# One transformer block with a 128 x 128 expert table: odd weight builds of the second half scaled by VectorE, two heads of u rows beside them, and routing pieces between the last tile's residual sums

## The chip, the cores and the metric

One core of a Trainium2 chip. TensorE (PE) multiplies matrices, VectorE (DVE) and ScalarE (ACT) work on rows of 128 partitions, GpSimd (POOL) issues the indirect gathers, SyncE (SP) issues the plain loads. The metric is device time in microseconds of one launch.

## The reference

Two blocks run on 512 tokens of width 1024. The first is pooling plus forgetting attention. The second is two attentions followed by an expert layer, `peer_ffn`, and the change lies in that layer:

```python
def block(xt):                                   # 128 tokens
    q = (xt @ w_q).reshape(128, 8, 2, 128)
    sc = einsum('thcd,chnd->thcn', q, sub_keys)  # 2 x 128 scores a head
    top_s, top_i = top_k(sc, 16)
    cand_s = top_s[:, :, 0, :, None] + top_s[:, :, 1, None, :]
    cand_i = top_i[:, :, 0, :, None] * 128 + top_i[:, :, 1, None, :]
    best_s, best_pos = top_k(cand_s.reshape(128, 8, 256), 16)
    idx = take_along_axis(cand_i..., best_pos)   # 16 of 16384 experts
    g = softmax(best_s)
    pre = einsum('td,thkd->thk', xt, u[idx])
    coef = g * gelu(pre)
    return einsum('thk,thkd->td', coef, v[idx])
```

Each token and head picks 16 experts, takes the dot product with their u rows, and sums their v rows with the weights `coef`. Everything is float32, so one gather of a row for 128 tokens moves 512 KB.

## The kernel before, in words

There are four tiles of 128 tokens and eight heads, so 32 chunks k = 8*tile + head, with 16 rows each. Two tiles at a time go through the dense layers and the attentions. Then the expert layer has its own stages.

**Routing.** `prep_top(k)` on VectorE finds the 16 experts of a chunk, in seven pieces with a `yield` after each. They are taken from one stream, `experts()`. In the attention code `side(n)` takes the next n pieces of the stream. `combine(i, n)` adds one of four projections to the residual of tile i, `prep_norm` norms it, and TensorE then projects the queries (the `pq` weights).

**Chunks 0 to 15 (tiles 0 and 1).** Their u rows are gathered and dotted (`dots`) during the dense work. Their v part is not gathered: TensorE multiplies the whole v table, 128 tiles of 128 rows, by a dense matrix of weights. The matrix is made in two halves of 64 tiles. For each half there are 32 builds. `picks(b)` on VectorE makes two one-hot operands for 8 tokens, `pick_a` (128 x 512) and `pick_j` (128 x 1024). ScalarE multiplies `pick_a` by the weights (`scaled`, eight instructions of 128 x 64). TensorE multiplies the two (`build`), and ScalarE copies the product out of PSUM (`spread`). Operands and PSUM banks are doubled: `picks(b)` waits for build b-2. After the 32 builds of a half, `dense(i)` runs its 64 tiles.

**Chunks 16 to 31 (tiles 2 and 3).** Their u and v rows are both gathered. GpSimd issues them in the fixed order `SEQ`, one queue, strictly in turn, and `wait_buffer` holds each until its buffer is free. Chunks 16 and later use a ring of 12 row buffers (`row_ring`), until v24. So a gather waits until the row twelve places ahead of it in the order has been used. A u row is freed by VectorE's dot product, a v row of chunks 16 and 17 by TensorE (`weighted`, with a diagonal made by ScalarE), a later v row below 24 by VectorE (`added`). From v24 on more buffers serve.

**Second half of the builds.** TensorE does one build and one v row of chunks 16 and 17 in turn, 32 of each. VectorE does `picks`, and in the first eight builds also two dots of u24. GpSimd's order is u24, v16, v17, u25, v18, u26, v19 and so on.

**After it.** VectorE walks `SEQ`. At each u chunk that is not in `WITH_SECOND` it first routes up to three more heads (`k_top < k + 5`), then does the dots. After every u chunk, also one in `WITH_SECOND`, it calls `weigh` for chunks up to k-2. `weigh(k)` waits for ScalarE's Exp and Gelu of that chunk, and ScalarE does the pair for chunk k at the place of u(k+1) in `SEQ`. So it does the pair of chunk 23 right after its last `spread` of the builds.

In the text below "build 40" means counting both halves, so the second half is builds 32 to 63. "v row 0 to 31" counts the rows of v16 and v17 together, and row n follows build 32+n.

## Time and profile before

| | us |
|---|---|
| median of 3 runs | 2355.33 |
| lowest, highest | 2352.23, 2360.59 |
| profiled execution | 2354.88 |
| its span, first to last instruction | 2353.0 |

So 1.88 us lie around the span. Busy over the span: PE 83%, DVE 63%, POOL 42%, ACT 23%, and the DMA engines move 261 GB/s on average. In 40 slices, each digit a tenth:

```profile
PE   6999999987498998987887799999899999503466
DVE  0111124453888884679974889988366867786644
DMA  5322335065487687797886773899774999999998
```

A slice is 59 us. The builds of the first half run at about 1346 to 1462, the first 64 tiles to 1684, the second builds to 1814, the last 64 tiles to 2031. After that only row gathers are left.

### The profile page before, as it was taken

Reading aid. Unit: us, or ns where it says so; the run is one execution under the profiler, and the core shown is the slowest. Engines: PE = TensorE matmul, PEld = TensorE weight load, DVE = VectorE, ACT = ScalarE, POOL = GpSimd, SP = SyncE. Lnnn points to the kernel's source line nnn. Section 1 sums busy time; section 2 is a strip of 40 time slices with the busy share of each in tenths; the row PEclk is TensorE's granted clock in tenths of the full one; section 3 lists DMA queues with packets and bytes.
Section 4 is the critical chain, followed back from the end, with each engine's and each line's share of the span. In section 5 each row is a group of like instructions: output and inputs, shape, how many; then the busy total and the mean of one; then the engine's idle time right before and its main releaser. Section 6 shows DMA issues by size and latency. Waiting matters only on the chain.

```text
span 2353.0 us, 22353 instructions
## 1 busy us (share of the span) xinstructions
PE 1961.2 (83%) x7682; PEld 1294.1 (55%) x7682; DVE 1474.5 (63%) x3261; ACT 531.2 (23%) x1476; POOL 986.1 (42%) x814
## 2 busy tenths in 40 slices
PE   6999999987498998987887799999899999503466
PEld 6777756576476665555665799444466444201122
DVE  0111124453888884679974889988366867786644
ACT  1011023322111110113431277110177000000111
POOL 2000000000244373466742342476262776687775
PEclk9899999698798888995599855999999999857899
DMA  5322335065487687797886773899774999999998
GB/s 160 108 90 90 121 116 179 18 224 205 153 302 261 215 302 297 265 400 264 274 300 248 272 261 101 321 394 409 267 239 154 371 409 409 410 363 367 380 377 359
DMA packets 190625, 614.86 MB, mean 261 GB/s; under 512 B 18096, under 2 KB 18096, under 8 KB 190512
## 3 DMA queue, kind: packets, MB, share of 16 engines
q0 software_dynamic: 111168, 403.64, 46.3%
q1 hardware_dynamic: 76400, 202.92, 23.4%
q10 hardware_dynamic: 2944, 6.89, 0.8%
q8 instruction: 61, 1.00, 0.2%
q14 instruction: 52, 0.43, 0.1%
HBM read 610.22 MB, written 3.15 MB: 261 GB/s over the span
## 4 chain that ended last, share of the span: by engine, by line
PE 51%; POOL 17%; DVE 12%; issue 10%; DMA 8%; ACT 2%; ACTq 0%; POOLq 0%; SPq 0%; DVEq 0%
PE ps L1669 50%; POOL sb_arena L638 14%; DVE sb_arena L1154 4%; POOL sb_wring L638 3%; DMA sb_arena<-in_peer_u,sb_idx 2%; DMA sb_arena<-in_peer_v,sb_idx 2%; DMA sb_wring<-in_peer_u,sb_idx 1%; DMA sb_wring<-in_w_out 1%; DMA sb_wring<-in_peer_v,sb_idx 1%; DMA sb_gains<-in_norm_g 1%; DVE sb_arena L1609 1%; DMA sb_wring<-in_w_in 1%; PE ps L1978 0%; DVE sb_arena L1615 0%; ACT sb_arena L873 0%
## 5 line engine op out<-in xcount | busy, mean ns | idle before, releaser
L638 POOL DMA_INDIRECT sb_arena<-in_peer_u,sb_idx x468 | 622.9, 1331 | 1165.3 <-DVE sb_idx L1144 540.9
L1669 PE MATMUL ps<-sb_wring,sb_arena 128*128 128x512 f32 (+2 forms) x1632 | 702.0, 591 | 33.0 <-DMA sb_wring<-in_w_out 10.7
L1154 DVE CUSTOM_DVE_ANT_0 sb_arena<-sb_arena 128x1024 f32<-128x1024 f32 x468 | 554.7, 1222 | 71.8 <-DMA sb_arena<-in_peer_u,sb_idx 68.8
L1669 PE MATMUL ps<-sb_arena,sb_wring 128*128 128x256 f32 (+2 forms) x2816 | 544.2, 356 | 47.0 <-issue 31.3
L1669 PEld LDWEIGHTS ps<-sb_wring,sb_arena 128*128 128x128 f32 x1632 | 313.7, 194 | 410.8 <-issue 367.2
L1669 PEld LDWEIGHTS ps<-sb_arena,sb_wring 128*128 128x128 f32 x2816 | 475.8, 204 | 103.3 <-issue 36.9
L1669 PE MATMUL ps<-sb_arena 128*128 128x64 f32 (+8 forms) x2016 | 400.1, 359 | 43.7 <-ACT sb_arena L897 11.4
L1669 PEld LDWEIGHTS ps<-sb_arena 128*128 128x128 f32 (+4 forms) x2016 | 329.6, 230 | 106.7 <-issue 61.0
L1669 PE MATMUL ps<-sb_arena,sb_poolw 128*128 128x512 f32 (+1 forms) x308 | 149.7, 611 | 153.1 <-DMA sb_arena<-in_peer_v,sb_idx 150.0
L638 POOL DMA_INDIRECT sb_arena<-in_peer_v,sb_idx x200 | 228.1, 1141 | 107.2 <-issue 51.8
L1183 DVE SCALAR_TENSOR_TENSOR sb_arena<-sb_arena,sb_coef 128x1024 f32<-128x1024 f32 x127 | 163.1, 1285 | 104.1 <-DMA sb_arena<-in_peer_v,sb_idx 99.2
L1669 PEld LDWEIGHTS ps<-sb_arena,sb_poolw 128*128 128x128 f32 x308 | 54.4, 195 | 228.9 <-issue 178.4
L1012 ACT ACTIVATE sb_arena<-sb_arena 128x64 f32<-128x64 f32 x512 | 128.9, 335 | 50.9 <-DVE sb_arena L1273 47.3
L1273 DVE TENSOR_TENSOR sb_arena<-sb_arena,sb_iota 128x512 f32<-128x512 f32 x64 | 44.2, 691 | 92.3 <-PE ps L1669 92.0
L980 ACT ACTIVATE sb_coef<-sb_coef 128x16 f32<-128x16 f32 (+1 forms) x18 | 4.0, 225 | 403.9 <-DVE sb_coef L1154 403.8
L1669 PE MATMUL ps<-sb_wring,sb_poolw 128*128 128x512 f32 x92 | 49.8, 669 | 43.5 <-ACT sb_poolw L1003 26.3
L1003 ACT ACTIVATE sb_poolw<-sb_ident,sb_coef 128x128 f32<-128x128 f32 x96 | 37.9, 400 | 200.3 <-PE ps L1669 200.3
L638 POOL DMA_INDIRECT sb_wring<-in_peer_v,sb_idx x56 | 66.1, 1180 | 32.3 <-issue 14.0
L1276 DVE TENSOR_TENSOR sb_arena<-sb_arena,sb_iota 128x1024 f32<-128x1024 f32 x64 | 77.9, 1218 | 0.0
L638 POOL DMA_INDIRECT sb_wring<-in_peer_u,sb_idx x44 | 56.6, 1287 | 45.8 <-PE ps L1669 27.7
L1407 DVE TENSOR_REDUCE sb_stat<-ps 128x1 f32<-128x144 f32 (+3 forms) x32 | 16.2, 505 | 91.7 <-PE ps L1669 91.5
L1154 DVE CUSTOM_DVE_ANT_0 sb_wring<-sb_wring,sb_arena 128x1024 f32<-128x1024 f32 x44 | 52.8, 1222 | 13.5 <-DMA sb_wring<-in_peer_u,sb_idx 13.4
(239 smaller groups left out, 1391.7 us busy)
## 6 DMA issues: line engine op xcount, KB each, us to landing
sb_wring<-in_peer_v SPq DMA_DIRECT2D x128, 512.0 KB, 6.8
sb_wring<-in_w_in SPq DMA_DIRECT2D x52, 1024.0 KB, 7.4
sb_wring<-in_peer_w_q SPq DMA_DIRECT2D x32, 1024.0 KB, 8.2
sb_wring<-in_w_o SPq DMA_DIRECT2D x16, 1024.0 KB, 7.2
sb_wring<-in_w_out SPq DMA_DIRECT2D x8, 1024.0 KB, 10.1
sb_arena<-in_peer_u,sb_idx POOLq DMA_INDIRECT x468, 6.9
sb_arena<-in_x ACTq DMA_DIRECT2D x8, 512.0 KB, 7.0
sb_wring<-in_w_up_pool SPq DMA_DIRECT2D x4, 1024.0 KB, 7.1
```

What stands on the lines that cost most here:

```text
L638: nc.gpsimd.indirect_dma_start(gathered[buf(n)], None, table, bass.IndirectOffsetOnAxis(ap=idx[:, t, at_:at_ + 1], axis=0))\
L980: nc.scalar.activation(coef[:, t, cols], coef[:, t, cols], ACT.Gelu).then_inc(gelu_done, k1 - k0)
L1003: nc.scalar.activation(diag[:, n % 4, :], ident[:], ACT.Copy, scale=coef[:, t, s:s + 1])\
L1012: last = nc.scalar.activation(pick_a[:, b % 2, n, :], pick_a[:, b % 2, n, :], ACT.Copy, scale=rank_t[:, 2 * TG + t, at_ + n:at_ + n + 1])
L1154: nc.vector.tensor_tensor_reduce(out=gathered[buf(n)], in0=gathered[buf(n)], in1=xn[:, t % TG, :], scale=1.0, scalar=0.0, op0=ALU.mult, op ...
L1183: nc.vector.scalar_tensor_tensor(rows_of_tile(t), gathered[buf(n)], coef[:, t, s:s + 1], rows_of_tile(t), ALU.mult, ALU.add).then_inc(vect ...
L1273: nc.vector.tensor_tensor(pick_a[:, b % 2], first_.to_broadcast([P, PICK, HALF]), iota[:, HALF * half:HALF * (half + 1)].unsqueeze(1) .to_ ...
L1276: nc.vector.tensor_tensor(pick_j[b % 2], second_.to_broadcast([P, PICK, NK]), iota[:].unsqueeze(1).to_broadcast([P, PICK, NK]), ALU.is_equal)\
L1407: nc.vector.tensor_reduce(stat[:, 96 + n % 4:97 + n % 4], s_ps[:, 0:w], AX, ALU.max, negate=True)\
L1609: link(nc.vector.tensor_tensor_scan(suffix[:, w - 1::-1] if w == T else suffix[:, 0:w][:, ::-1], suffix[:, w - 1::-1] if w == T else suffi ...
L1669: return nc.tensor.matmul(o, l, r, start=start, stop=stop)
```

## The change

- `by_vector(b)`: in the second half the odd builds have their `pick_a` multiplied by VectorE, one instruction with a broadcast weight. The even builds and the first half stay with ScalarE. TensorE's `build` waits for the semaphore of whoever did it.
- Chunk u25 moves beside the builds: GpSimd's order becomes u24, v16, u25, v17, u26, v18, ..., u30, v22, v23. VectorE does two dots in each of the first eight builds (u24) and one in each of the next sixteen (u25).
- The last tile's `combine` calls have two pieces of the stream between them, in all six.
- Head 19 is routed ahead of the first builds, where it was routed among them. In its place dots of chunk 18 stand between these builds.

```diff
+        def by_vector(b):
+            return b >= BUILDS and b % 2 == 1
...
-        BESIDE = [("b", 0), ("u", 24), ("v", 16), ("v", 17)]
-        LATER = [item for k in range(25, 31) for item in (("u", k), ("v", k - 7))]
+        BESIDE = [("b", 0), ("u", 24), ("v", 16), ("u", 25), ("v", 17)]
+        LATER = [item for k in range(26, 31) for item in (("u", k), ("v", k - 8))] + [("v", 23)]
...
-        WITH_FIRST, WITH_SECOND = (16, 17, 18), (24,)
+        WITH_FIRST, WITH_SECOND = (16, 17, 18), (24, 25)
...
-                        if b + 1 < BUILDS:
+                        if b + 1 < BUILDS and not by_vector(BUILDS + b + 1):
                             scaled(BUILDS + b + 1)
...
-                third_rows = dots(18)
-                between = chain(first_rows, dots(17), tops_of(19), third_rows)
+                yield from tops_of(19)
+                between = chain(first_rows, dots(17), dots(18))
...
                             picks(BUILDS + b)
-                            for _ in range(2):
-                                next(between, None)
+                            if by_vector(BUILDS + b):
+                                scaled(BUILDS + b)
+                            next(between, None)
+                            if b < TOPK // 2:
+                                next(between)
...
+            def scaled(b):
+                t, at_ = divmod(b % BUILDS * PICK, P)
+                dve.wait_ge(pick_ones, b + 1)
+                weight_ = rank_t[:, 2 * TG + t, at_:at_ + PICK].unsqueeze(2)
+                nc.vector.tensor_tensor(pick_a[:, b % 2], pick_a[:, b % 2], weight_.to_broadcast([P, PICK, HALF]),
+                                        ALU.mult).then_inc(dve_scaled, 1)
...
                 for n in range(4):
+                    if n and g:
+                        side(2)
                     combine(i, n)
...
-                pe.wait_ge(pick_scaled, b + 1)
+                pe.wait_ge(dve_scaled if by_vector(b) else act_scaled,
+                           sum(by_vector(m) == by_vector(b) for m in range(b + 1)))
```

**GpSimd's queue beside the second builds.** `u_used` counts VectorE's dots, `v_used` TensorE's v rows. Before, from the last part of u24 on (v16, v17, u25):

```order
L638 DMA sb_arena<-in_peer_u,sb_idx 128x1024 [waits u_used] x8
L638 DMA sb_arena<-in_peer_v,sb_idx 128x1024 [waits u_used] x2
L638 DMA sb_wring<-in_peer_v,sb_idx 128x1024 [waits u_used] x2
L638 DMA sb_arena<-in_peer_v,sb_idx 128x1024 [waits u_used] x8
L638 DMA sb_arena<-in_peer_v,sb_idx 128x1024 [waits v_used] x2
L638 DMA sb_wring<-in_peer_v,sb_idx 128x1024 [waits v_used] x2
L638 DMA sb_arena<-in_peer_v,sb_idx 128x1024 [waits v_used] x10
L638 DMA sb_wring<-in_peer_v,sb_idx 128x1024 [waits v_used] x2
L638 DMA sb_arena<-in_peer_v,sb_idx 128x1024 [waits v_used] x4
L638 DMA sb_arena<-in_peer_u,sb_idx 128x1024 [waits v_used,idx_ready]
```

The same place with the change, from v16's last four rows on (then u25, then v17):

```order
L642 DMA sb_arena<-in_peer_v,sb_idx 128x1024 [waits v_used] x2
L642 DMA sb_wring<-in_peer_v,sb_idx 128x1024 [waits v_used] x2
L642 DMA sb_arena<-in_peer_u,sb_idx 128x1024 [waits v_used,idx_ready]
L642 DMA sb_arena<-in_peer_u,sb_idx 128x1024 [waits v_used] x9
L642 DMA sb_wring<-in_peer_u,sb_idx 128x1024 [waits v_used] x2
L642 DMA sb_arena<-in_peer_u,sb_idx 128x1024 [waits u_used] x4
L642 DMA sb_arena<-in_peer_v,sb_idx 128x1024 [waits u_used] x6
L642 DMA sb_wring<-in_peer_v,sb_idx 128x1024 [waits u_used] x2
```

The sixteen gathers of u25 now stand between v16 and v17, and twelve of them wait for v rows 4 to 15.

**VectorE at builds 39 to 41 of the second half.** The L1273 and L1276 rows are `picks`, a pair of L1154 rows is one dot (`gathered` names its row buffer). Before:

```order
L1273 TENSOR_TENSOR sb_arena<-sb_arena,sb_iota 128x512 [waits pick_used]
L1276 TENSOR_TENSOR sb_arena<-sb_arena,sb_iota 128x1024
L1154 ISA sb_arena,sb_coef<-sb_arena 128x1024 [waits gathered12]
L1154 ISA sb_coef 128x1
L1154 ISA sb_arena,sb_coef<-sb_arena 128x1024 [waits gathered13]
L1154 ISA sb_coef 128x1
L1273 TENSOR_TENSOR sb_arena<-sb_arena,sb_iota 128x512 [waits pick_used]
L1276 TENSOR_TENSOR sb_arena<-sb_arena,sb_iota 128x1024
L1273 TENSOR_TENSOR sb_arena<-sb_arena,sb_iota 128x512 [waits pick_used]
L1276 TENSOR_TENSOR sb_arena<-sb_arena,sb_iota 128x1024
```

With the change, builds 40 and 41 (`picks` is now L1288 and L1291, the multiplication L1276, a dot L1158):

```order
L1291 TENSOR_TENSOR sb_arena<-sb_arena,sb_iota 128x1024
L1158 ISA sb_arena,sb_coef<-sb_arena 128x1024 [waits gathered14]
L1158 ISA sb_coef 128x1
L1288 TENSOR_TENSOR sb_arena<-sb_arena,sb_iota 128x512 [waits pick_used]
L1291 TENSOR_TENSOR sb_arena<-sb_arena,sb_iota 128x1024
L1276 TENSOR_TENSOR sb_arena<-sb_arena 128x512 [waits pick_ones]
L1158 ISA sb_arena,sb_coef<-sb_arena 128x1024 [waits gathered15]
L1158 ISA sb_coef 128x1
```

A dot of u25, with its wait for a gathered row, now stands between the operands of one build and those of the next.

**VectorE after the last build.** Before:

```order
L1163 RECIPROCAL sb_pstat<-sb_pstat 128x1 [waits soft_exp]
L1165 SCALAR_TENSOR_TENSOR sb_coef<-sb_coef,sb_pstat,sb_soft 128x16 [waits gelu_done,dve_chain]
L1097 MAX sb_arena<-sb_wring 128x8 [waits prep_evac]
L1097 MAX sb_arena<-sb_wring 128x8
L1100 MAX_INDEX sb_arena<-sb_arena,sb_wring 128x8 [waits dve_chain]
```

With the change:

```order
L1167 RECIPROCAL sb_pstat<-sb_pstat 128x1 [waits soft_exp]
L1169 SCALAR_TENSOR_TENSOR sb_coef<-sb_coef,sb_pstat,sb_soft 128x16 [waits gelu_done,dve_chain]
L1167 RECIPROCAL sb_pstat<-sb_pstat 128x1 [waits soft_exp]
L1169 SCALAR_TENSOR_TENSOR sb_coef<-sb_coef,sb_pstat,sb_soft 128x16 [waits gelu_done,dve_chain]
L1101 MAX sb_arena<-sb_wring 128x8 [waits prep_evac]
```

`weigh(23)` has moved ahead of the routing of heads 28 and 29, and head 30 follows them directly, where dots stood between.

## Rows read from the trace of the kernel before

**Rows 1.** Windows: stretch, length, busy us of each engine (instructions), clock, DMA share.

```profile
core 0: us, PE busy (x) PEld busy (x) DVE busy (x) ACT busy (x) POOL busy (x), PEclk, DMA share, GB/s
1684.30:1813.70 129.40, 116.50 (x642) 83.45 (x641) 74.60 (x117) 86.47 (x304) 53.56 (x43) 0.93 0.55 178
1826.40:2031.00 204.60, 204.60 (x478) 90.61 (x477) 152.18 (x251) 9.27 (x15) 144.67 (x109) 1.00 1.01 402
2031.00:2117.50 86.50, 2.57 (x6) 0.78 (x5) 76.88 (x97) 4.47 (x10) 69.75 (x55) 0.53 0.99 379
2117.50:2353.00 235.50, 129.81 (x256) 45.87 (x256) 132.32 (x132) 29.83 (x70) 172.01 (x160) 0.86 0.96 370
```

**Rows 2.** Timeline, PE from 1694 to 1814: start, length, instruction, [idle before <- releaser].

```profile
1694.44 3.75 PE L1669 MATMUL ps<-sb_arena,sb_poolw 128*128 128x512 f32 x4 [8.23 <-DMA sb_arena<-in_peer_v,sb_idx]
...
1708.35 3.75 PE L1669 MATMUL ps<-sb_wring,sb_poolw 128*128 128x512 f32 x4 [4.67 <-DMA sb_wring<-in_peer_v,sb_idx]
...
1719.08 1.89 PE L1669 MATMUL ps<-sb_arena 128*128 128x64 f32 x16
1720.81 1.94 PE L1669 MATMUL ps<-sb_arena,sb_poolw 128*128 128x512 f32 x4
...
1813.67 16.90 PE L1669 MATMUL ps<-sb_wring,sb_arena 128*128 128x512 f32 x39
```

**Rows 3.** Timeline, VectorE and ScalarE around and after the second builds.

```profile
1726.10 0.68 DVE L1273 TENSOR_TENSOR sb_arena<-sb_arena,sb_iota 128x512 f32<-128x512 f32 x1
...
1752.54 0.69 DVE L1273 TENSOR_TENSOR sb_arena<-sb_arena,sb_iota 128x512 f32<-128x512 f32 x1 [1.68 <-PE ps L1669]
...
1806.84 0.16 DVE L1163 RECIPROCAL sb_pstat<-sb_pstat 128x1 f32<-128x1 f32 x1
...
1824.89 1.22 DVE L1154 CUSTOM_DVE_ANT_0 sb_arena<-sb_arena 128x1024 f32<-128x1024 f32 x1
...
1815.62 0.21 ACT L980 ACTIVATE sb_coef<-sb_coef 128x16 f32<-128x16 f32 x1
```

**Rows 4.** Timeline, POOL's gathers beside and after the second builds.

```profile
1725.30 1.68 POOL L638 DMA_INDIRECT sb_arena<-in_peer_v,sb_idx  x1 [0.60 <-DVE sb_coef L1154]
...
1735.72 1.95 POOL L638 DMA_INDIRECT sb_arena<-in_peer_v,sb_idx  x1 [0.30 <-issue]
...
1754.55 0.94 POOL L638 DMA_INDIRECT sb_wring<-in_peer_v,sb_idx  x1 [1.63 <-PE ps L1669]
...
1826.39 1.68 POOL L638 DMA_INDIRECT sb_arena<-in_peer_u,sb_idx  x1 [11.34 <-DVE sb_coef L1154]
```

**Rows 5.** Tile view, gathers: issue to landing at 1774 to 1815, then 1735 to 1754.

```profile
DMA to landing us min/median/max: 3.9/4.1/5.3
...
DMA to landing us min/median/max: 5.2/5.9/6.4
```

**Rows 6.** Timeline, the last tile's residual sums to the second build: DVE, PE, POOL.

```profile
1284.45 0.75 DVE L1581 SCALAR_TENSOR_TENSOR sb_arena<-ps,sb_stat,sb_arena 128x512 f32<-128x512 f32 x1 [2.60 <-PE ps L1669]
...
1295.63 0.09 DVE L1103 MATCH_VALUE_LOAD sb_arena<-sb_arena 128x8 f32 x1
...
1345.63 0.68 DVE L1273 TENSOR_TENSOR sb_arena<-sb_arena,sb_iota 128x512 f32<-128x512 f32 x1
...
1351.80 1.22 DVE L1154 CUSTOM_DVE_ANT_0 sb_wring<-sb_wring,sb_arena 128x1024 f32<-128x1024 f32 x1 [4.35 <-DMA sb_wring<-in_peer_u,sb_idx]
...
1320.36 9.46 PE L1669 MATMUL ps<-sb_arena,sb_wring 128*128 128x128 f32 x56 [3.38 <-DMA sb_wring<-in_peer_w_q]
...
1335.15 6.52 PE L1669 MATMUL ps<-sb_arena,sb_wring 128*128 128x128 f32 x56 [3.55 <-DMA sb_wring<-in_peer_w_q]
...
1355.79 16.45 PE L1669 MATMUL ps<-sb_arena 128*128 128x64 f32 x76 [3.62 <-issue]
...
1303.78 0.94 POOL L638 DMA_INDIRECT sb_arena<-in_peer_u,sb_idx  x1 [40.67 <-DVE sb_idx L1144]
...
1343.84 1.17 POOL L638 DMA_INDIRECT sb_wring<-in_peer_u,sb_idx  x1 [21.65 <-PE ps L1669]
```

More of the change, by code:

```diff
@@ L256, in build @@
         rank_ready = sem("rank_ready"); rank_mm = sem("rank_mm"); rank_copied = sem("rank_copied")
-        pick_ones = sem("pick_ones"); pick_done = sem("pick_done"); pick_scaled = sem("pick_scaled"); pick_used = sem("pick_used"); spread_done = sem("spread_done")
+        pick_ones = sem("pick_ones"); pick_done = sem("pick_done"); act_scaled = sem("act_scaled"); dve_scaled = sem("dve_scaled"); pick_used = sem("pick_used"); spread_done = sem("spread_done")
         d_used = sem("d_used")
@@ L1013, in scaled @@
                                                 scale=rank_t[:, 2 * TG + t, at_ + n:at_ + n + 1])
-                last.then_inc(pick_scaled, 1)
+                last.then_inc(act_scaled, 1)
             def spread(b):
```

## The prediction

> **What bounds the kernel now.** I read the windows first, then the timeline of each engine where two stages meet. [rows 1] cut the end of the span into four. In the second builds (129.4 us) the DMA engines are busy 0.55 of the time. Then comes a stretch of 204.6 us with PE full (the last 64 tiles) and DMA at 1.01, in which POOL issues 109 gathers, one per 1.88 us. Then 55 gathers in 86.5 us, one per 1.57, with PE idle. The last 235.5 us begin with the gathers of v23. So from about 1826 us on the transfers set the end, and PE sets when that stretch may start. In the second builds PE is the bound: from build 37 at 1719.08 to the tiles at 1813.67 there are 27 builds with their rows, 3.50 us each, without a gap [rows 2]. The only gaps are two waits for gathered v rows, 8.23 and 4.67 us, each followed by a group that took 3.75 us where the later one took 1.94 [rows 2]. VectorE waits 1.68 us per build for PE there [rows 3]. So ScalarE's multiplications are not what PE waits for, and taking half of them away gives no time. What the change can win is the 16 rows of u25, moved from a stage that is full to one that is half empty.
>
> **Part 1, before and in the first builds.** The gaps between the residual sums are 2.60 us [rows 6]. Six pieces of head 16 fill them; the same pieces took 7.8 us after 1295.63, three gaps' worth, so they cost no more than some tenths there. Head 16's rows were issued from 1303.78, after 40.67 us of POOL idle [rows 6]. They now start about 12 us earlier, when fewer of the query weights are on their way, and PE's waits for those weights, 3.38 and 3.55 us [rows 6], should mostly go. VectorE's way to the first picks loses 7.8 us and up to 2.5 us of waits for rows, and gains head 19. A head costs (1824.89 - 1806.84 - 0.4)/2 = 8.8 us [rows 3]. So the first picks, at 1345.63 before, come 1 to 1.5 us earlier. Then the next wait: VectorE stood 4.35 us for a row in a weight buffer, issued at 1343.84 when PE had finished the projections, and build 1 came 3.62 us late [rows 6]. PE finishes some 6 us earlier now, the row has landed when it is asked for, and that wait goes. Sum -5 us at the start of the first 64 tiles, which PE does back to back. Bounds: -7, and +3 if the early rows hold the weights back instead.
>
> **Part 2, the second builds.** The multiplication on VectorE, 128 x 512, costs about 0.69 us by the nearest row of that size [rows 3], in 16 builds. VectorE has 1.68 us free per build after build 40; 16 dots of 1.2 and a multiplication in every second one fit into it on average, hardly in the odd ones. By itself this would cost PE 1 us. The waits for rows are the larger part.
>
> The ring has 12 buffers. *First place, build 40.* The first dot of u25 stands between the picks of 40 and 41. Its gather is the one that follows v row 15 in POOL's queue, so it takes the place of the gather at 1735.72 [rows 4]. VectorE is at that dot at 1726.10 + 1.9 + 1.2 for two multiplications = 1729. POOL is then still busy with v rows 12 to 15, and even if these go a little faster with VectorE idle, the row is issued at about 1735.3. It lands 4.1 to 5.9 us later [rows 5], 1739.4 to 1741.2. Dot, picks and multiplication, 1.2 + 1.9 + 0.7, put build 41 at 1743.2 to 1745.0. It was due at 1719.08 + 4 x 3.50 = 1733.1. That is 10.1 to 11.9 us, I take 11, and 1.8 us for a slow group behind the gap (3.75 against 1.94, as behind the two gaps of [rows 2]).
>
> *Second place, v row 16.* Twelve rows ahead of u25's row 11 stands v row 15. PE finishes it when build 48 is due, 1719.08 + 11 x 3.50 = 1757.6. Only then can POOL issue u25 rows 11 to 15, and then v row 16, which PE wants 1.7 us later. Before, that row was in its buffer long since, issued at 1735.72. Five gathers take 1.24 us each with VectorE idle (0.94 and 0.30), 2.25 with VectorE busy (1.95 and 0.30), and 18.8/11 = 1.7 on average from 1735.72 to 1754.55 [rows 4]. With five at 1.6 and 4.9 to land the row is there 12.9 us after its release: a wait of 11 us, bounds 5 x 1.24 + 4.1 - 1.7 = 8.6 and 5 x 2.25 + 5.9 - 1.7 = 15.5. With the slow group 12.8.
>
> Together +26 us for this stage, bounds 20 and 32. Once these two are over VectorE is again ahead, since its rows are then issued four builds before they are asked for.
>
> The landing time can be weighed against the Trainium skill, page "DMA: Bandwidth & Descriptors", section "Anatomy of one DMA — SWDGE (gpsimd) path": about 2.0 us fixed and the bytes at 436 GB/s. That would be an estimate of 3.2 us for 512 KB where [rows 5] have 4.1 and 5.9. By it both waits would be 1 to 2 us shorter and the time 2363; the rows decide.
>
> **Part 3, after the builds.** In both versions twelve u rows are gathered ahead when the builds end, and POOL stands until VectorE's first dot. Before, POOL went on at 1826.39 [rows 4], 12.7 us after PE's last build group ended at 1813.67. VectorE had left the builds at 1806.84 and routed two heads. Now weigh(23) stands ahead of the heads, and needs the Gelu that ScalarE ends at 1815.8, which is 2.2 us after PE's end [rows 3]; then three heads in a row. POOL goes on at 2.2 + 0.2 + 3 x 8.8 + 1.5 = 30.3 us after PE's end, 17.6 us later than before. Gathers to issue from there to v23: 109 + 55 = 164 before, 148 now, since u25 is out. In the tiles' stretch (204.6 - 17.6)/1.88 = 99.5 fit, and 48.5 are left, at 1.57 us 76.3 against 86.5 us. So of the 16 x 1.57 = 25 us that 16 rows are worth at that rate, 10 us are left: -10. Bounds: -17 if the lost time is partly made up (DMA was half busy in it anyway), -7 if the third head's delay costs more.
>
> **Sum.** 2354.88 (the profiled execution, 0.5 under the median) - 5 + 26 - 10 = 2366 us.
>
> **Rivals.** Around its median this kernel can be told from no change only by more than 0.3%, 7 us: faster is below 2348.3, slower above 2362.4.
>
> *A, the forecast,* 2366 us, range 2352 to 2379, of which a fifth lies below 2362.4.
>
> *B, the gathers land in time and the row count wins.* If VectorE and PE lead POOL by less than I read, so that the dot of u25's row 0 and v row 16 find their rows, part 2 is +1 and the time is 2354.9 - 5 + 1 - 10 = 2341, faster. It is decided by whether five or six gathers behind the release fit into the slack of one or two builds. For it: POOL and DMA are half idle there [rows 1]. Against it: one gather alone is 1.24 us and 4.1 to land, more than one build's 3.50, and before the change the same mechanism cost the 8.23 and 4.67 us of [rows 2].
>
> *C, shorter waits.* Both waits at their lower ends (-6) and a tail worth its upper bound (-7): 2353, the same.
>
> *D, the shared port.* A gather's issue is 0.94 us with VectorE idle and 1.68 to 1.95 beside it [rows 4]. The change puts 16 dots and 16 multiplications beside 44 gathers. If all are slow, the second wait is 3.3 us longer, and with its slow groups twice as long as taken the stage gives +33: 2373. The Trainium skill, page "SBUF — State Buffer", section "SBUF: two separate sides", has GpSimd locked out of the shared port pair by some VectorE instructions while it writes descriptors. By that rule this is where the time would go.
>
> **How the numbers follow.** A 0.65, B 0.07, C 0.18, D 0.10. Slower: 0.8 x 0.65 + 0.10 = 0.62. Same: 0.13 + 0.18 = 0.31. Faster: 0.07. The range 2348 to 2379 leaves out B and the ends of A and D, under two in ten.
>
> **What would show it.** In the profile after: the first dot of head 16's rows and the first tiles about 5 us earlier; in the second builds one wait of VectorE for a u row of 9 to 11 us with PE late behind it, at build 41, and one wait of PE for a v row of 9 to 15 us at build 48; 155 us for the stage; POOL idle some 29 us after it, with VectorE waiting for ScalarE; then 48 or 49 gathers after the last tile. It would be wrong if PE showed no gap at 41 and 48, if the stretch after the builds restarted early, or if the early rows delayed the query weights.

## The result and the profile after

| | before | changed | ratio, 95% interval |
|---|---|---|---|
| median of 9 runs each, us | 2359.80 | 2377.44 | 1.0057, 1.0029 to 1.0085 |
| lowest, highest | 2352.23, 2373.84 | 2363.40, 2384.99 | |
| profiled execution | 2354.88 | 2364.46 | |
| its span | 2353.0 | 2362.5 | |

The change makes the kernel slower by 0.57%, which is 13.4 us of 2359.8 (7 to 20 by the interval); the two medians are 17.6 us apart. The prediction's 2366 lies 10.7 us above the median it started from. The profiled execution of the changed kernel is the second lowest of its nine times, and its span is only 9.5 us longer than that of the kernel before.

The windows of the changed kernel, cut where [rows 1] are cut: second builds, from POOL's restart to the same place in the last tiles, the u rows behind it, and the end. A "u row" or "v row" is one gather of 128 rows of the table, "granted clock" (PEclk) the clock that TensorE got as a share of its full 2.4 GHz.

```profile
core 0: us, PE busy (x) PEld busy (x) DVE busy (x) ACT busy (x) POOL busy (x), PEclk, DMA share, GB/s
1674.20:1833.70 159.50, 122.50 (x641) 86.74 (x640) 95.33 (x133) 57.80 (x184) 71.59 (x59) 0.85 0.58 197
1864.10:2051.00 186.90, 186.90 (x437) 83.02 (x436) 132.36 (x194) 9.27 (x15) 115.07 (x98) 1.00 1.01 398
2051.00:2128.60 77.60, 2.63 (x7) 0.84 (x5) 69.25 (x89) 1.42 (x5) 61.30 (x51) 0.54 1.00 385
2128.60:2362.50 233.90, 130.14 (x256) 46.11 (x256) 132.19 (x126) 29.84 (x70) 170.35 (x160) 0.86 0.97 371
```

The second builds take 159.5 us where [rows 1] have 129.4, with almost the same TensorE work, at a granted clock of 0.85 on average instead of 0.93. The stretch with full tiles is 17.7 us shorter, since POOL restarts later, and the next one 8.9 us shorter, since fewer gathers are left.

PE's waits in the second builds, grouped by what ended them (total us, times, longest):

```profile
PE ps L1687 <- DMA sb_arena<-in_peer_v,sb_idx: 20.0, 2, 11.8
PE ps L1687 <- DVE sb_arena L1291: 11.4, 1, 11.4
PE ps L1687 <- DMA sb_wring<-in_peer_v,sb_idx: 5.3, 1, 5.3
```

The two waits of [rows 2], 8.2 and 4.7 us, are still there as 8.15 and 5.25. The two new ones are 11.38 and 11.84. Their places, PE's timeline:

```profile
1735.69 3.65 PE L1687 MATMUL ps<-sb_arena 128*128 128x64 f32 x16 [11.38 <-DVE sb_arena L1291]
1739.12 3.73 PE L1687 MATMUL ps<-sb_arena,sb_poolw 128*128 128x512 f32 x4
1742.64 2.29 PE L1687 MATMUL ps<-sb_arena 128*128 128x64 f32 x16
...
1777.79 3.55 PE L1687 MATMUL ps<-sb_arena,sb_poolw 128*128 128x512 f32 x4 [11.84 <-DMA sb_arena<-in_peer_v,sb_idx]
```

The first is build 41, the second v row 16. Three groups behind the first gap run slow, 3.65, 3.73 and 2.29 us where 1.90, 1.94 and 1.90 are usual, and one behind the second. On VectorE, ahead of build 41:

```profile
1718.33 1.22 DVE L1291 TENSOR_TENSOR sb_arena<-sb_arena,sb_iota 128x1024 f32<-128x1024 f32 x1
1732.01 1.23 DVE L1158 CUSTOM_DVE_ANT_0 sb_arena<-sb_arena 128x1024 f32<-128x1024 f32 x1 [12.46 <-DMA sb_arena<-in_peer_u,sb_idx]
...
1733.76 1.22 DVE L1291 TENSOR_TENSOR sb_arena<-sb_arena,sb_iota 128x1024 f32<-128x1024 f32 x1
1734.90 0.69 DVE L1276 TENSOR_TENSOR sb_arena<-sb_arena 128x512 f32<-128x512 f32 x1
```

VectorE has finished build 40's operands at 1719.55 and then stands 12.46 us at the first dot of u25. The operands of build 41 are behind that dot in its program. POOL at the two places, and after the builds:

```profile
1725.64 0.94 POOL L642 DMA_INDIRECT sb_arena<-in_peer_u,sb_idx  x1 [0.31 <-issue]
...
1764.50 1.23 POOL L642 DMA_INDIRECT sb_wring<-in_peer_u,sb_idx  x1 [1.73 <-PE ps L1687]
1766.04 0.94 POOL L642 DMA_INDIRECT sb_arena<-in_peer_u,sb_idx  x1 [0.31 <-issue]
...
1771.50 0.94 POOL L642 DMA_INDIRECT sb_arena<-in_peer_v,sb_idx  x1 [0.30 <-issue]
...
1864.15 1.68 POOL L642 DMA_INDIRECT sb_arena<-in_peer_u,sb_idx  x1 [29.05 <-DVE sb_coef L1158]
```

The row for that dot is issued at 1725.64, behind the last rows of v16. At the second place row 11 of u25 is released when v row 15 is done (1764.50); four more rows of u25 follow, and v row 16 comes out at 1771.50. The tile views of these two gathers give 6.3 to 6.4 us and 6.2 us from issue to landing:

```profile
DMA to landing us min/median/max: 6.3/6.4/6.4
...
DMA to landing us min/median/max: 6.2/6.2/6.2
```

The restart at 1864.15 stands 30.4 us behind PE's last build group. VectorE shows why, in the place of the reciprocal of [rows 3]:

```profile
1834.40 0.16 DVE L1167 RECIPROCAL sb_pstat<-sb_pstat 128x1 f32<-128x1 f32 x1 [6.47 <-ACT sb_soft L976]
1835.99 0.23 DVE L1169 SCALAR_TENSOR_TENSOR sb_coef<-sb_coef,sb_pstat,sb_soft 128x16 f32<-128x16 f32 x1 [1.44 <-ACT sb_coef L984]
```

It waits for ScalarE's Exp and Gelu of chunk 23, then routes three heads, and only then frees a buffer.

### The profile page after: what moved, and what is told of

The parts are those of the page before. It is cut to its first block, busy times and chain, and to the rows that moved or that the text cites. A ratio compares the mean times of both kernels' runs of the same rounds, so it can differ in the third digit from the quotient of the medians.

```text
span 2362.5 us, 22238 instructions
## 1 busy us (share of the span) xinstructions
PE 1959.3 (83%) x7682; PEld 1293.0 (55%) x7682; DVE 1483.3 (63%) x3277; ACT 500.7 (21%) x1348; POOL 963.7 (41%) x814
## 4 chain that ended last, share of the span: by engine, by line
PE 56%; POOL 13%; DMA 11%; DVE 9%; issue 9%; ACT 2%; ACTq 0%; POOLq 0%; SPq 0%; DVEq 0%
PE ps L1687 55%; POOL sb_arena L642 10%; DMA sb_arena<-in_peer_v,sb_idx 5%; DVE sb_arena L1158 3%; DMA sb_arena<-in_peer_u,sb_idx 3%; POOL sb_wring L642 3%; DMA sb_wring<-in_w_out 1%; DMA sb_gains<-in_norm_g 1%; DMA sb_wring<-in_w_in 1%; DVE sb_arena L1624 1%; PE ps L1996 1%; DMA sb_wring<-in_w_up_attn 0%; ACT sb_arena L877 0%; DVE sb_arena L1630 0%; DVE sb_stat L1609 0%
## 5 line engine op out<-in xcount | busy, mean ns | idle before, releaser
L1158 DVE CUSTOM_DVE_ANT_0 sb_arena<-sb_arena 128x1024 f32<-128x1024 f32 x468 | 555.3, 1222 | 82.0 <-DMA sb_arena<-in_peer_u,sb_idx 79.0
L642 POOL DMA_INDIRECT sb_arena<-in_peer_v,sb_idx x200 | 221.2, 1106 | 118.8 <-DVE sb_coef L1158 60.7
L1016 ACT ACTIVATE sb_arena<-sb_arena 128x64 f32<-128x64 f32 x384 | 96.8, 335 | 62.8 <-DVE sb_arena L1288 58.7
L1288 DVE TENSOR_TENSOR sb_arena<-sb_arena,sb_iota 128x512 f32<-128x512 f32 x64 | 44.4, 693 | 87.0 <-PE ps L1687 87.0
L1291 DVE TENSOR_TENSOR sb_arena<-sb_arena,sb_iota 128x1024 f32<-128x1024 f32 x64 | 78.0, 1219 | 0.0
L642 POOL DMA_INDIRECT sb_wring<-in_peer_v,sb_idx x56 | 59.4, 1060 | 37.2 <-DVE sb_coef L1158 21.3
L1027 ACT COPY sb_arena<-ps 128x512 f32<-128x512 f32 x64 | 37.4, 584 | 140.0 <-PE ps L1687 140.0
```

What stands on the lines that cost most here:

```text
L642: nc.gpsimd.indirect_dma_start(gathered[buf(n)], None, table, bass.IndirectOffsetOnAxis(ap=idx[:, t, at_:at_ + 1], axis=0))\
L1016: last = nc.scalar.activation(pick_a[:, b % 2, n, :], pick_a[:, b % 2, n, :], ACT.Copy, scale=rank_t[:, 2 * TG + t, at_ + n:at_ + n + 1])
L1027: nc.scalar.copy(dense_w[:, :, t, at_:at_ + PICK], psum[:, 4 + b % 2, :].rearrange("p (s i) -> p i s", s=PICK)).then_inc(spread_done, 1)
L1158: nc.vector.tensor_tensor_reduce(out=gathered[buf(n)], in0=gathered[buf(n)], in1=xn[:, t % TG, :], scale=1.0, scalar=0.0, op0=ALU.mult, op ...
L1288: nc.vector.tensor_tensor(pick_a[:, b % 2], first_.to_broadcast([P, PICK, HALF]), iota[:, HALF * half:HALF * (half + 1)].unsqueeze(1) .to_ ...
L1291: nc.vector.tensor_tensor(pick_j[b % 2], second_.to_broadcast([P, PICK, NK]), iota[:].unsqueeze(1).to_broadcast([P, PICK, NK]), ALU.is_equal)\
```

## The experiments

The reasons to be tested: (a) the two waits come from the order of the gathers, u25's sixteen rows as one block between v16 and v17, and not from the number of rows; (b) the late restart comes from `weigh(23)` and three heads in a row; (c) VectorE's multiplications neither cost nor give. The main rival is that the additional transfers, or VectorE's work beside POOL's, slow the stage whatever the order. The runs were made in three groups, each group on one chip with its own runs of the kernel before, so ratios are to these.

### u25 put back, and u25 alone

`e1_u25_back` is the changed kernel with u25 behind the builds again:

```diff
-        BESIDE = [("b", 0), ("u", 24), ("v", 16), ("u", 25), ("v", 17)]
-        LATER = [item for k in range(26, 31) for item in (("u", k), ("v", k - 8))] + [("v", 23)]
+        BESIDE = [("b", 0), ("u", 24), ("v", 16), ("v", 17)]
+        LATER = [item for k in range(25, 31) for item in (("u", k), ("v", k - 7))]
-        WITH_FIRST, WITH_SECOND = (16, 17, 18), (24, 25)
+        WITH_FIRST, WITH_SECOND = (16, 17, 18), (24,)
```

> The changed kernel with chunk u25 put back to its old place in the gather order and out of the second builds; the multiplications on VectorE, the pieces between the residual sums and head 19's place stay as changed. Theory (the order of the gathers in a ring of 12 makes the two waits): the second builds take 130 to 131 us instead of 159.6, with no wait at build 41 and none at v row 16, POOL restarts 12 to 14 us after them, and the whole is 2 to 4 us faster than before (ratio 0.998 to 0.999). Rival (VectorE's extra work beside the builds makes PE late): the second builds stay above 140 us although u25 is gone, and the kernel stays slower than before.

Measured 1.0007 (0.9984 to 1.0030), so the gain of 2 to 4 us isn't seen. The second builds take 130.7 us, with waits of 8.46 and 5.49 us and none at build 41 or v row 16, and POOL goes on after 13.3 us. The slowdown goes with u25.

`e2_u25_alone` is the kernel before with only the move of u25 (the same lines the other way round, and one dot a build after the eighth); ScalarE multiplies everything:

> The kernel before with only u25 moved beside the second builds (gather order, dots, nothing else; ScalarE scales all builds). Theory: both waits are there, 10 to 12 us each, the second builds take 155 to 159 us, POOL restarts 30 us after them, and the kernel is 16 to 20 us slower than before (ratio 1.007 to 1.009). Rival (the multiplications on VectorE carry a good part): under 145 us for the stage and a ratio under 1.004.

Measured 1.0091 (1.0063 to 1.0120). The second builds take 163.2 us, and VectorE waits at the same dot:

```profile
1743.24 1.22 DVE L1154 CUSTOM_DVE_ANT_0 sb_arena<-sb_arena 128x1024 f32<-128x1024 f32 x1 [12.73 <-DMA sb_arena<-in_peer_u,sb_idx]
```

PE's new waits are 11.38 and 12.93 us, and POOL goes on 30.4 us after the builds. So the move alone makes the whole loss, here 21 us where 16 to 20 were expected. Its stage is even 3.7 us longer than the changed kernel's.

### The same rows in another order

`e4_rows_in_turn` is the changed kernel with the gathers of u25 and of v rows 8 to 31 row by row, in the order in which they are used. No gather and no instruction of another engine is added or taken away:

```diff
+        first_ = place["v", 16]
+        at_row = {("v", 16, j): first_ + j for j in range(8)}
+        n_ = first_ + 8
+        for j in range(24):
+            if j < 16:
+                at_row["u", 25, j] = n_
+                n_ += 1
+            m_ = j + 8
+            at_row["v", 16 + m_ // TOPK, m_ % TOPK] = n_
+            n_ += 1
...
-                    n = place["u", k] + j
+                    n = row_place("u", k, j)
```

> The changed kernel with the gathers of v16, u25 and v17 issued row by row in the order in which they are used: v rows 0 to 7, then one of u25 and one v row in turn, then the last 8 v rows. VectorE, ScalarE and TensorE do exactly what they do in the changed kernel. Theory (queue order): both waits go, the second builds take 130 to 132 us, POOL still restarts 30 us after them, and the kernel is 27 us faster than the changed one: 10 to 14 us faster than before (ratio 0.994 to 0.996). Rival (VectorE's load, or the landing of rows in a busier stage): PE keeps at least 10 us of new waits in the second builds, and the ratio stays above 1.

Measured 0.9932 (0.9903 to 0.9961), a little better than the 0.994 to 0.996 expected. PE's waits in the second builds of this kernel:

```profile
PE ps L1705 <- DMA sb_arena<-in_peer_v,sb_idx: 8.4, 1, 8.4
PE ps L1705 <- DMA sb_wring<-in_peer_v,sb_idx: 5.4, 1, 5.4
PE ps L1705 <- issue: 0.4, 1, 0.4
```

Both new waits are gone, and the stage is 131.1 us with all its 59 gathers:

```profile
1696.90:1828.00 131.10, 116.81 (x641) 83.22 (x640) 95.17 (x133) 57.71 (x184) 82.14 (x59) 0.93 0.71 239
```

Against the changed kernel's window the gathers (x59), VectorE's instructions (x133) and TensorE's (x641) are the same numbers, and the DMA share is higher, 0.71 against 0.58. Sixteen more gathers beside the work don't slow this stage; their order does. This settles (a).

### The restart after the builds

`e6_rows_weigh` is the kernel of the last section with one more edit, and `e5_weigh_later` is the changed kernel with this edit alone: `weigh(23)` stands behind the dots of u26.

```diff
-                        while k_w <= (CHUNKS - 1 if k == CHUNKS - 1 else k - LAG):
+                        while k != 25 and k_w <= (CHUNKS - 1 if k == CHUNKS - 1 else k - LAG):
```

> As the kernel with the rows in turn, and weigh(23) is not called at the place of u25 but two calls later, after the dots of u26. Theory: VectorE starts head 28 some 8.2 us sooner after the builds, POOL restarts 21 to 22 us after them instead of 30, 8.4/1.88 = 4.5 gathers more fit beside the tiles, and that is worth 4.5 x 1.57 = 7 us on top of the rows in turn (ratio 0.991 to 0.993). Rival (DMA makes good what it lost, since it is the bound on both sides): 0 to 2 us.

> The changed kernel with one edit: weigh(23) stands after the dots of u26 instead of ahead of the routing. The order of the gathers stays. My theory: VectorE starts its three heads without waiting for ScalarE, GpSimd goes on about 22 us after the last build instead of 30.4, the second builds keep their length of 159.6 us and both waits at 41 and 48. The 8 us of earlier restart are 8/1.88 = 4.4 gathers more beside the tiles, 4.4 x 1.57 = 7 us: ratio to the changed kernel about 0.997, to the kernel before 1.002 to 1.004. Rival: the rows missed are made up anyway, since the DMA engines were half busy there, and the time stays at 1.0057.

e6 measured 0.9894 (0.9866 to 0.9921). By the ratios that is 9 us under e4, by the medians of the same group 9.8 (2331.27 against 2341.09); 7 were expected. POOL goes on 22.1 us after the builds, after an idle time of 20.53:

```profile
1835.88 1.68 POOL L660 DMA_INDIRECT sb_arena<-in_peer_u,sb_idx  x1 [20.53 <-DVE sb_coef L1176]
```

e5 measured 1.0042 (1.0015 to 1.0068). Its stage is 159.8 us with both waits (11.35 and 11.98), and its restart also comes at 22.1 us. That is 1.5 thousandths or 3.5 us under the changed kernel's 1.0057, about half of what was expected and within both intervals; on its own it shows no gain. The pair e4 and e6 shows one: their intervals still overlap, but five of e4's seven times lie above all six of e6, and a sixth above all but one. The place of the restart is shown by both pairs: without `weigh(23)` ahead of the heads it comes 8.3 us sooner (22.1 against 30.4). What an earlier restart is worth rests on e4 and e6 alone.

`e8_head_beside` adds to e6 the routing of head 28 in the last eight builds:

```diff
-                        between = chain(*[dots(k_) for k_ in WITH_SECOND])
+                        between = chain(*[dots(k_) for k_ in WITH_SECOND], tops_of(k_top))
+                        k_top += 1
```

> The rows in turn, weigh(23) after u26's dots, and in addition head 28 routed in the last eight second builds, one piece in each, where VectorE has no dots. My theory, that the restart of GpSimd after the builds is worth 1.57/1.88 of its time: second builds stay at 131 us, GpSimd goes on 13 us after the last build instead of 22, 9/1.88 = 4.8 more gathers beside the tiles, 7.5 us less than the kernel without this edit (which had 0.9894): ratio 0.986 to 0.987. Rival: a piece of 1.25 us and a multiplication of 0.35 don't fit VectorE's 1.7 us there, and the builds become 3 to 5 us longer, ratio 0.988 to 0.990.

Measured 0.9896 (0.9855 to 0.9937). The stage stays at 130.3 us, so the pieces fit, and POOL goes on after 14.3 us, 7.8 us sooner for one head less. This settles (b) for the time of the restart. But the ratio is that of e6, not 0.003 less. It came from another chip, where the end of every trace is longer (below), and its interval is wide: the gain isn't shown here.

### Who multiplies

`e7_act_scales` is the changed kernel, and `e9_rows_act` is e6, with ScalarE multiplying in all builds (`by_vector` returns False). `e6_again` is e6 once more, in the group of e9.

> The changed kernel with ScalarE multiplying the operands of all builds, as before the change. My theory, that the multiplications on VectorE carry nothing: second builds of 158 to 161 us with the same waits at builds 41 and 48, the wait at build 41 shorter or longer by 1 us at most, ratio to the kernel before 1.005 to 1.008. Rival: VectorE's multiplications cost time beside the gathers (longer issues, 1.7 to 2 us against 1.2), then the wait for v row 16 falls by some 3 us and the ratio is 1.003 or less.

> The kernel with the rows in turn and weigh(23) after u26's dots once more, as the measure for the three others of this group. Expected: second builds of 131 us, GpSimd going on 22 us after the last build, ratio to the kernel before 0.987 to 0.992. Where it falls outside, the ratios of different groups can't be compared at this size.

> As e6_again, but ScalarE multiplies the operands of every build. With the changed kernel's own order of gathers this exchange cost 4 us in the second builds (163.45 against 159.56). My theory: VectorE's multiplication shortens only the way from a late u row to its build, so with no late row it is worth nothing: stage 130 to 132 us, ratio within 0.002 of e6_again. Rival: it shortens every build, stage 134 us or more.

e7 measured 1.0080 (1.0047 to 1.0113), with a stage of 163.45 us and waits of 11.6 and 13.1 us. e6_again measured 0.9920 (0.9891 to 0.9950), e9 0.9936 (0.9911 to 0.9961), with stages of 131.2 and 130.2 us. Where no row is late, the exchange is worth nothing in the stage. Where rows are late it saves 3.7 us of it (163.45 against 159.76 in e5, on the same chip): 1.1 in the wait for v row 16 and 3.0 in the slow groups behind it, with small differences both ways elsewhere. Behind that wait e7 has

```profile
1794.08 3.75 PE L1687 MATMUL ps<-sb_arena,sb_poolw 128*128 128x512 f32 x4 [13.07 <-DMA sb_arena<-in_peer_v,sb_idx]
1797.62 3.51 PE L1687 MATMUL ps<-sb_arena 128*128 128x64 f32 x16
1800.93 3.09 PE L1687 MATMUL ps<-sb_arena,sb_poolw 128*128 128x512 f32 x4
```

where e5 has one of 3.47 and the changed kernel one of 3.55. So (c) holds only where no row is late. Why the groups stay slow longer isn't settled.

### The pieces and head 19 alone

`e3_pieces_alone` is the kernel before with the change's other part, `side(2)` between the residual sums and head 19 ahead of the first builds.

> The kernel before, with only the pieces between the last tile's residual sums and head 19 ahead of the first builds (dots of chunk 18 between them). My theory: the first 64 tiles start 3 to 5 us earlier, the second builds are as before (129 to 131 us, two waits of 8 and 5 us), and GpSimd goes on 12 to 13 us after the last build. Since the run with u25 put back, which has this part too, showed an earlier start and no gain in the time, I expect a ratio of 0.997 to 1.000 here. Rival: the earlier start is worth its 3.5 us in full, ratio 0.9985 or less in the middle.

Measured 0.9995 (0.9971 to 1.0019). Together with e1's 1.0007 no gain is seen. On the first chip there are, from the last residual sum to the second builds, 389.5 to 390.5 us in the four traces with the pieces (the changed kernel, e1, e4, e6), and 394.1 in e2 and 393.0 in the kernel before without, so some 3 to 4 us are there in that stretch. This is 0.0015 of the time, less than either interval can tell. e3's own trace can't show it: it has 396.3 us there, with a wait of VectorE for ScalarE of 8.55 us that every trace of the other two chips has and none of the first (last section), and no kernel without the pieces was profiled on these chips.

### A version from these findings

The first two waits of the stage, 8.2 and 4.7 us in [rows 2], are in every kernel so far. POOL stands 28 to 33 us there for a dot of u24 that VectorE has only behind the operands of the next build, and VectorE stands 27 to 33 us for PE. `e10_ahead_act` takes e9 and puts all dots of u24 ahead of the builds; heads 28 and 29 are routed in the builds instead. `e11_ahead_both` has the odd builds multiplied by VectorE besides.

```diff
-                        between = chain(*[dots(k_) for k_ in WITH_SECOND])
+                        yield from dots(24)
+                        between = chain(tops_of(k_top), dots(25), tops_of(k_top + 1))
+                        k_top += 2
...
-                            if b < TOPK // 2:
-                                next(between)
```

> As e9_rows_act, but all sixteen dots of u24 stand ahead of the second builds, where VectorE idles 31 us at their door; heads 28 and 29 are routed in the builds in place of these dots, one piece in each of the first seven and of seven later ones. My theory: the gathered rows of v16 no longer wait for dots in the builds, so the two waits of 8.3 and 5.2 us at the second and fourth build go, with their slow groups of 3.7 us: the stage is 113 to 116 us, GpSimd goes on under 8 us after the last build. From the tail's slope of 1.75 us a row, 14 us of earlier restart are worth 7 rows, 12 us. Ratio to e6_again 0.988 to 0.992 (16 us from the builds, of which the tail gives some back since fewer gathers fit beside the work), in the middle 0.990. Rival: the end of the kernel is set by the number of gathers alone, and a shorter stage of builds with no gathers more in it is given back in full, then the ratio to e6_again is 0.996 or more.

> As e10_ahead_act, with the odd builds multiplied by VectorE as in the changed kernel. VectorE's own work is then 1.9 + 0.35 + 1.25 = 3.5 us a build, as much as TensorE's 3.5. My theory: it becomes a second bound and the stage is 1 to 4 us longer than that of e10_ahead_act, ratio 0.000 to 0.002 above it. Rival: the queue of two builds evens it out and both are the same.

e10 measured 0.9790 (0.9746 to 0.9834), 2325.10 us against 2377.23; e11 0.9813 (0.9777 to 0.9849). The second builds of e10, then the tiles from about the restart on:

```profile
1693.30:1805.40 112.10, 112.10 (x641) 81.50 (x640) 94.85 (x190) 86.84 (x306) 60.84 (x47) 1.00 0.77 262
1813.20:2025.30 212.10, 212.10 (x495) 93.60 (x493) 148.05 (x219) 14.23 (x26) 137.03 (x114) 1.00 1.02 405
```

PE is busy for all of the 112.1 us, at a granted clock of 1.00, its 2.4 GHz level: 32 times 3.50, so nothing but its own work is left in the stage. POOL goes on after 3.9 us:

```profile
1809.30 1.68 POOL L660 DMA_INDIRECT sb_arena<-in_peer_u,sb_idx  x1 [2.52 <-DVE sb_coef L1176]
```

The ratio to e6_again is 0.987 from the two ratios, with an interval (estimated from theirs) of about 0.005 either way; 0.988 to 0.992 was expected. The rival, that a shorter stage is given back at the end, is out. The stage of e11 is 112.1 us too, so the expected second bound on VectorE is not there; that the lead of two builds evens it out fits this, but was not tested by itself. Its ratio lies within e10's interval. Both kernels beat the two compared ones.

### What the end of the kernel follows

| kernel | second builds, us | POOL goes on, us after | rows gathered after the last tile | from the builds to the end, us |
|---|---|---|---|---|
| before | 129.4 | 12.7 | 213 | 539.3 |
| e1_u25_back | 130.7 | 13.3 | 214 | 540.2 |
| changed | 159.6 | 30.4 | 207 | 528.8 |
| e4_rows_in_turn | 131.2 | 30.4 | 207 | 523.8 |
| e2_u25_alone | 163.2 | 30.4 | 207 | 518.8 |
| e6_rows_weigh | 131.0 | 22.1 | 202 | 516.8 |
| *another chip:* e3_pieces_alone | 129.6 | 12.7 | 213 | 555.4 |
| e7_act_scales | 163.5 | 30.4 | 208 | 546.5 |
| e5_weigh_later | 159.8 | 22.1 | 202 | 535.4 |
| e8_head_beside | 130.3 | 14.3 | 198 | 530.3 |
| *a third chip:* e6_again | 131.2 | 22.1 | 202 | 542.8 |
| e9_rows_act | 130.2 | 21.6 | 202 | 528.1 |
| e10_ahead_act | 112.1 | 3.9 | 193 | 520.9 |
| e11_ahead_both | 112.1 | 4.5 | 194 | 527.0 |

Between the traces with 213 or 214 rows and the three with 207 lie 15.9 us on the mean, 2.4 a row; from e3 to e8, on one chip, 15 rows give 25.1 us, 1.7 a row. The single traces scatter by 5 us around this on the first chip (three kernels with 207 rows). On the third chip they scatter by 14.7 us at the same 202 rows (e6_again and e9), twice what lies between e9 and e10 with nine rows fewer. So fewer rows left go with a shorter end in the first two groups, the third can't show it, and the slope is known only roughly.

## Why the prediction was right, point by point

**Part 1, -5 forecast.** The second builds begin at 1674.17 instead of 1684.31, 10.1 us earlier. But the last residual sum (1284.63, before 1291.32) is already 6.7 us earlier, and so is the first (1274.41, before 1281.10), ahead of every piece. This is a difference between two executions: in the traces of all these programs, which are the same up to there, the first sum begins anywhere from 1274.4 to 1296.1. What is left, -3.4 us, is inside the bounds. Two details were wrong. Only one of the waits for query weights went; the other is 4.40 us. And the wait for the row in a weight buffer halved instead of going:

```profile
1314.68 9.15 PE L1687 MATMUL ps<-sb_arena,sb_wring 128*128 128x128 f32 x56 [4.40 <-DMA sb_wring<-in_peer_w_q]
...
1341.28 1.23 DVE L1158 CUSTOM_DVE_ANT_0 sb_wring<-sb_wring,sb_arena 128x1024 f32<-128x1024 f32 x1 [2.14 <-DMA sb_wring<-in_peer_u,sb_idx]
```

PE finished the projections some 3 us earlier, net of the shared 6.7, not 6, so the row's issue (1334.03) moved less than I took.

**Part 2, +26 forecast, +30.2 found.** Both places are where they were put, and the waits have the size: 11.38 and 11.84 us against 11 and 11. The step that was mis-sized is the price of the slow groups: I took 1.8 us behind each gap, and the first cost 3.9 (1.75, 1.79 and 0.39 over the usual), the second 1.6. The first two waits together are 0.5 us longer. The sum 11.4 + 3.9 + 11.8 + 1.6 + 0.5 + 0.4 for a small gap at build 40 is 29.6 of the 30.2. The mean granted clock of 0.85 against 0.93 goes with it.

At build 41 two errors cancel. Counted from the start of the stage, the row was issued 51.5 us in (51.0 forecast), but it landed 6.3 us later, above the bounds of 4.1 to 5.9, and build 41 began 0.8 us later than the late end of its forecast. It was also due 1.3 us later than forecast, so the wait came out at 11.4.

Behind v row 16 two errors cancel. Five gathers were issued in 7.0 us, 1.4 each (1.6 taken), and the landing took 6.2 (4.9 taken), in all 13.3 from release to use (12.9). The Trainium skill's page "DMA: Bandwidth & Descriptors", section "Anatomy of one DMA — SWDGE (gpsimd) path", gave an estimate of 3.2 us. The trace disagrees: the rows show 6.2 to 6.4, twice that, with five and more gathers in a row.

The multiplications cost PE next to nothing, as taken, but they are not without effect where rows are late: e7 shows they save 3.7 us there. The forecast had taken the exchange as worth no time.

**Part 3, -10 forecast.** From PE's last build to the end: 528.8 us against 539.3, so -10.5. POOL's restart was put at 30.3 us and came at 30.4, with VectorE waiting for ScalarE as described. There are 98 gathers in the full stretch (99.5 worked out) and 51 behind it (48.5), in 77.6 us (76.3). The agreement to half a microsecond is luck: in traces with the same restart and the same 207 rows it is -15.5 (e4) and -20.5 (e2).

**The sum.** -3.4 + 30.2 - 10.5 = +16.3, less the shared 6.7, is the 9.6 us between the two traces. The forecast parts sum to +11. The ratio makes the difference 13.4 us and the medians 17.6. But the stage was mis-sized by 4 us and the end scatters by 10. The mechanism was right; how close the number came is in part luck.

**The rivals.** *B*, that the rows land in time and their number wins, was put at 2341 us. It is false for the order that the change wrote. For the rows in turn it is borne out: e4 has a median of 2341.09 against 2355.33. What was said to decide it, how many gathers stand between a release and the row that is wanted, is what e4 changed. *C*, shorter waits, is out: both are at or over the value taken. *D*, the shared port, is out as the cause of the loss: the gathers of the second place took 0.94 to 1.43 us behind the first one, and e4 runs 59 gathers beside the same VectorE work in 131.1 us. Issues beside dots are longer all the same (1.68 at the restart, then 1.99), but in this stage they had room. The Trainium skill's page "SBUF — State Buffer", section "SBUF: two separate sides", would have them longer, by a port pair that VectorE and GpSimd share. The trace agrees in kind, but no run here shows that the port is the reason.

## What to carry to other kernels

With one in-order queue and a ring of buffers, write down for each transfer which use, one ring length (here twelve places) ahead, releases it, and how many transfers stand between that release and the row that is wanted next; here a block of sixteen rows put between two consumers cost a full release, issue and landing at both its ends, though the DMA engines were half idle. Interleave the rows in the order of their use before concluding that a stage has no room, and look at each idle engine in front of a stage: the largest gain here (18 us of stage) was work that could be done while two engines stood 30 us for a third. Taking rows out of a full stage pays even when the queue restarts late (e4, 0.9932 with the restart at 30.4 us), and more when it restarts sooner (e6, 0.9894 at 22.1), so what stands ahead of the first release after the stage is worth counting instruction by instruction.

## What was not expected of the hardware

**Idle times of about 10 us on some chips.** From the last tile on, the traces of the first group (and of the two compared kernels) have one ScalarE gap over 8 us ahead of a diagonal (the weights that TensorE needs for a v row), 73 to 91 us right behind the tile. Each trace of the other two groups, both on other chips, has that one and seven to nine more (71 to 94 us in all), of 8.0 to 11.5 us, with no releaser in the kernel. ScalarE in e6_again, the same program as e6_rows_weigh:

```profile
2293.12 0.40 ACT L1025 ACTIVATE sb_poolw<-sb_ident,sb_coef 128x128 f32<-128x128 f32 x1 [10.22 <-remote]
2304.34 0.40 ACT L1025 ACTIVATE sb_poolw<-sb_ident,sb_coef 128x128 f32<-128x128 f32 x1 [10.83 <-remote]
2315.61 0.40 ACT L1025 ACTIVATE sb_poolw<-sb_ident,sb_coef 128x128 f32<-128x128 f32 x1 [10.86 <-issue]
```

and the windows over these gaps (e6_again) and over the like stretch of e6_rows_weigh, in this order:

```profile
2290.00:2330.00 40.00, 14.60 (x16) 4.82 (x17) 19.27 (x15) 2.39 (x6) 26.27 (x27) 0.59 0.98 384
```

```profile
2264.00:2304.00 40.00, 29.41 (x62) 10.23 (x61) 19.72 (x16) 6.02 (x15) 30.55 (x32) 1.00 1.03 410
```

TensorE waits for each diagonal and falls to the lower of its two clock levels (a matmul takes 0.91 us instead of 0.47, the granted clock of the stretch is 0.59), and the end comes 542.8 us after the builds instead of 516.8. The kernel before is also slower on these chips (2379.17 and 2377.23 against 2355.33 us), so the ratios nearly cancel it (0.9894 and 0.9920 for one program). What the gaps are isn't settled; the DMA engines are at 0.98 there, and the instruction queues moved the same number of packets in both traces (62 and 51), which does not point to more loading of code. They stand ahead of the first builds too. In all eight traces of these two groups, and in none of the first, ScalarE idles 8.3 to 9.3 us there in six to eight pieces without a releaser, TensorE 5 to 6 us in the same stretch, and VectorE then waits 8.5 to 8.7 us for ScalarE's Gelu. In e3, ScalarE and VectorE:

```profile
1306.32 1.28 ACT L980 ACT_TABLE_LOAD   x1 [4.78 <-issue]
...
1308.03 0.23 DVE L1165 SCALAR_TENSOR_TENSOR sb_coef<-sb_coef,sb_pstat,sb_soft 128x16 f32<-128x16 f32 x1 [8.55 <-ACT sb_coef L980]
```

Each group was on one chip only, so whether the chip or something else of the group makes them is open. Spans of different groups can't be compared to 1%.

**Landing depends on what is issued around it.** The same 512 KB gather landed in 3.9 to 5.3 us in one stretch of [rows 5], 5.2 to 6.4 in another, and 6.2 to 6.4 at both places that mattered here.

**The price of a gap on TensorE is more than the gap.** The stage of e10 without gaps has a granted clock of 1.00; with two gaps it is 0.93, with four 0.85. Behind a gap of 11 to 13 us one to three groups took up to twice their time.
